# A two-block transformer kernel on one core: attention mask by short products, recurrent splits and mixes moved, first unit of three feed-forward stages reordered

## The reference

```python
for layer in range(2):
    if layer == 1:
        k_shared, v_shared = shared_kv(x, ...)
    x = x + 0.5 * swiglu(rmsnorm(x, ffn1_norm[layer]), w_gate, w_up, w_down)    # 1024 -> 2816 -> 1024
    h = rmsnorm(x, mix_norm[layer])
    if layer == 0:
        x = x + recurrent_block(h, ...)
    else:
        x = x + diff_attention(h, k_shared, v_shared, ...)
    x = x + 0.5 * swiglu(rmsnorm(x, ffn2_norm[layer]), w_gate, w_up, w_down)

def recurrent_block(h, ...):
    gate, rec = split(h @ w_in)
    rec = rg_lru(causal_depthwise_conv(rec))      # h_t = a_t h_{t-1} + bx_t
    return (gelu(gate) * rec) @ w_out

def diff_attention(...):                          # 8 heads, each with two score maps
    scores = q @ k.T                              # blocks of 128 queries
    mask = key // 64 <= query // 64
    p = softmax(where(mask, scores, -inf))
    attn = p[:, 0] - lam * p[:, 1]
    return rmsnorm(attn @ v) @ w_o
```

## Time and profile before

| | us |
|---|---|
| median of 3 executions (3706.11 to 3715.54) | 3709.11 |
| the profiled execution, whole | 3714.02 |
| its span, first to last instruction | 3712.7 |
| PE busy in the span | 3600.5 |
| DVE busy | 2471.0 |
| ACT busy | 1601.6 |
| POOL busy | 288.2 |
| mean granted clock of PE | 0.977 of full speed |

### The profile page before, as it was taken

How to read it: one execution, slowest core, us unless ns; L and a number is a source line. 1 busy time by engine, 2 the same in 40 slices (tenths; PEclk the granted TensorE clock), 3 DMA queues, 4 the chain that set the end, 5 groups by cost and what they waited for, 6 DMA issues and landing times.

```text
span 3712.7 us, 53317 instructions
## 1 busy us (share of the span) xinstructions
PE 3600.5 (97%) x21504; PEld 3067.0 (83%) x21504; DVE 2471.0 (67%) x3699; ACT 1601.6 (43%) x2579; POOL 288.2 (8%) x245
## 2 busy tenths in 40 slices
PE   8999999999999998999999999999999999979999
PEld 5866788888888866888899986899978999659998
DVE  6455767755547265544688877888756887478886
ACT  3246733323135234422454446544444444475443
POOL 0001005820000011000000011000020000110000
PEclk8999999999999899999999999999999999999999
DMA  6200032333322101222333322233323334203332
GB/s 227 96 23 1 2 103 88 128 126 125 125 78 75 57 29 57 91 97 97 97 96 104 109 91 78 87 105 103 105 87 126 108 103 148 64 18 103 104 105 89
DMA packets 276455, 338.96 MB, mean 91 GB/s; under 512 B 15601, under 2 KB 197489, under 8 KB 275569
## 3 DMA queue, kind: packets, MB, share of 16 engines
q1 hardware_dynamic: 272752, 320.40, 27.5%
q10 hardware_dynamic: 3456, 15.14, 1.1%
HBM read 329.19 MB, written 6.29 MB: 90 GB/s over the span
## 4 chain that ended last, share of the span: by engine, by line
PE 82%; DVE 7%; ACT 2%; issue 2%; DMA 0%; POOL 0%; SPq 0%; ACTq 0%; DVEq 0%
PE ps L862 15%; PE ps L864 15%; PE ps L863 15%; PE ps L1788 7%; PE ps L1790 7%; PE ps L1789 7%; PE ps L2274 1%; PE ps L2248 1%; PE ps L2133 1%; PE ps L2134 1%; PE ps L2135 1%; DVE t L443 1%; PE ps L2238 1%; PE ps L877 1%; PE ps L879 1%
## 5 line engine op out<-in xcount | busy, mean ns | idle before, releaser
L862 PE MATMUL ps<-t 128*128 128x512 f32 (+1 forms) x2188 | 789.9, 361 | 4.0 <-DVE t L3840 2.7
L863 PE MATMUL ps<-t 128*128 128x512 f32 (+1 forms) x2188 | 785.6, 359 | 0.0
L864 PE MATMUL ps<-t 128*128 128x512 f32 (+1 forms) x2188 | 784.5, 359 | 0.0
L430 ACT ACTIVATE t<-t 128x1024 fp32r<-128x1024 f32 (+2 forms) x438 | 437.1, 999 | 566.6 <-PE ps L864 331.1
L443 DVE TENSOR_TENSOR t<-t 128x1024 fp32r<-128x1024 f32 (+2 forms) x438 | 505.8, 1156 | 244.3 <-ACT t L430 241.7
L1788 PE MATMUL ps<-blocks_hi,t 128*128 128x256 f32 x1888 | 533.0, 282 | 15.0 <-ACT t L1817 11.7
L1790 PE MATMUL ps<-blocks_hi,t 128*128 128x256 f32 x1888 | 528.6, 280 | 0.0
L1789 PE MATMUL ps<-blocks_lo,t 128*128 128x256 f32 x1888 | 528.6, 280 | 0.0
L862 PEld LDWEIGHTS ps<-t 128*128 128x128 f32 x2188 | 418.7, 191 | 67.3 <-issue 4.0
L863 PEld LDWEIGHTS ps<-t 128*128 128x128 f32 x2188 | 418.8, 191 | 60.2 <-issue 1.0
L864 PEld LDWEIGHTS ps<-t 128*128 128x128 f32 x2188 | 418.2, 191 | 60.7
(11 more groups left out here) (514 smaller groups left out, 6326.0 us busy)
## 6 DMA issues: line engine op xcount, KB each, us to landing
t<-w_s_up SPq DMA_DIRECT2D x184, 256.0 KB, 3.6
t<-w_up SPq DMA_DIRECT2D x88, 512.0 KB, 3.6
raw_more<-w_s_up SPq DMA_DIRECT2D x168, 256.0 KB, 3.4
t<-w_ada SPq DMA_DIRECT2D x160, 256.0 KB, 3.1
raw_more<-w_s_down SPq DMA_DIRECT2D x72, 256.0 KB, 2.7
t<-w_down SPq DMA_DIRECT2D x32, 512.0 KB, 3.6
t<-w_s_down SPq DMA_DIRECT2D x56, 256.0 KB, 2.7
t<-w_ada SPq DMA_DIRECT2D x16, 512.0 KB, 11.0
```

Source lines behind the costliest of these rows:

```text
L430: k.A.activation(self.pair(n)[0], self.slot(self.raw_at[n])[:, 0:self.size(n)], ACT.Copy)\
L862: k.T.matmul(out, wh, hh, start=(i == 0), stop=False)
L863: k.T.matmul(out, wh, hl, start=False, stop=False)
L864: ins = k.T.matmul(out, wl, hh, start=False, stop=(i == len(kts) - 1))
```

## The change

1. Attention: the memset and its semaphore go. After the two score products PE adds two short products into the corner of each map: 64 rows by 64 columns, a constant 0/1 matrix cut from the constants (`early_rows`) times a column of -2^94 read 64 times, which adds -2^100 for queries 0 to 63. The ratio is a `scalar_tensor_tensor` in place of a `tensor_scalar` with two scalars from memory.
2. Recurrent stage, i from 9: `dve_scans` gives a new order, in which the splits of chunks 13 to 17 and the last norms come between single scans; the split of chunk 13 on ACT lies between the two square roots; all mixes but the first move behind the last projection, each ahead of one low part, and the last two `dve_normed` (14 and 15) go there too. `rec_out` takes the paired form.
3. Blocks of the first unit in s_up10, s_up20 and s_up21 (s_up11 is not `summed` and keeps its order). DVE at tile 6: sum S2 comes right behind t1, the residual of tile 7 ahead of `dve_add(5)`; at tile 7 the differences first, then S2's low part, spans 2 and 1, `dve_add(6)`; in the stage itself A12's low part ahead of `dve_add(7)`. ACT: S2's high part right behind tile 6's square; `act_keep(0, 0)` ahead of span 1's high part; then A12's, the square of tile 7 and a small Sqrt activation that loads the table ahead of the root.

```diff
@@ -1269,8 +1270,6 @@
         k, (p, odd) = self.k, divmod(m, 2)
         for t in free:
             k.act.wait_ge(t)
-        if m == 6 and self.summed:
-            k.stream.split_hi(self.first)
         k.act.wait_ge(self.finished(m, 0))
         k.act.wait_ge(self.at("beside", 4 * p))
         k.act.wait_ge(self.low(p - 1, 1 if odd else 0))
@@ -1280,17 +1279,18 @@
             self.act_hi(p, 1)
         elif odd:
             self.act_hi(p, 2)
-            if self.summed:
-                k.stream.split_hi(self.first + 2)
-            self.act_hi(p, 1)
         else:
             if p:
                 self.act_hi(p - 1, 2)
             self.act_hi(p, 0)
             if m == 6 and self.summed:
                 k.stream.split_hi(self.first + 1)
-        if self.summed:
+        if self.summed and m < 7:
             self.act_square(m)
+        if m == 6 and self.summed:
+            k.stream.split_hi(self.first + 2)
+        if m == 7 and not self.summed:
+            self.act_hi(p, 1)
...
-    def dve(self, m, free=()):
+    def dve(self, m, free=(), last=None):
         k, st, (p, odd) = self.k, self.k.stream, divmod(m, 2)
         for t in free:
             k.dve.wait_ge(t)
         if not self.summed:
             self.dve_blocks(m)
+            if last:
+                last()
         elif m == 7:
+            self.dve_t234(p)
+            st.split_lo(self.first + 2)
+            self.dve_lo(p, 2)
+            self.dve_lo(p, 1)
             self.dve_add(6)
-            self.dve_t234(p)
-            st.sum(self.up, 0, "S2")
-            self.dve_lo(p, 2)
-            st.split_lo(self.first + 2)
-            self.dve_lo(p, 1)
         elif odd:
             self.dve_add(m - 1)
             self.dve_t234(p)
             self.dve_lo(p, 1)
-        else:
-            if m == 6:
-                st.sum(self.up, 0, "S1")
-            elif m:
+        elif m < 6:
+            if m:
                 self.dve_add(m - 1)
             self.dve_t1(p)
-            if m == 6:
-                st.split_lo(self.first)
             self.dve_lo(p, 0)
-            if m == 6:
-                st.split_lo(self.first + 1)
             if p:
                 self.dve_lo(p - 1, 2)
-            if m == 6:
-                self.dve_add(m - 1)
+        else:
+            st.sum(self.up, 0, "S1")
+            self.dve_t1(p)
+            st.sum(self.up, 0, "S2")
+            self.dve_lo(p, 0)
+            self.dve_lo(p - 1, 2)
+            st.split_lo(self.first + 1)
+            last()
+            self.dve_add(5)
...
+                if isinstance(feed, BlockFeed) and g == 2 and j == 7:
+                    feed.dve(6, [vd.at(ns * FT)], lambda: dve_residual(g, j))
+                    continue
...
                             act_silu(j, 0)
                         if j == 0 and q == 3 and source.summed:
                             source.act_root()
+                        if j == 0 and q == 0 and source.summed:
+                            act_keep(0, 0)
+                            source.act_hi(3, 1)
                         st.split_hi(st.look(c + q))
+                        if j == 0 and q == 0 and source.summed:
+                            source.act_square(7)
+                            k.A.activation(k.SM[:, 103:104], k.eps(EPS), ACT.Sqrt)
                         if j == 0 and q == 4 and source.summed:
                             source.act_rstd()
-                        if q < 3:
+                        if q < 3 and not (j == 0 and q == 0 and source.summed):
                             act_keep(j, q)
                         if q == 0 and left is not None:
...
                         if q > 3:
                             dve_even(j, q)
                         if j == 0 and q == 0 and source.summed:
+                            st.split_lo(c + 3)
                             source.dve_add(7)
                         if q == 0:
                             st.split_lo(c + 1)
...
+            if isinstance(self.feed, BlockFeed) and m == 7:
+                self.feed.dve(6, (), lambda: self.dve_residual(7))
+                continue
...
                     k.act.wait_ge(m2.at(4 * half + 4))
                     k.A.activation(v, v, ACT.Sqrt).then_inc(mu.sem, 1)
+                    if half == 0:
+                        st.split_hi(c0 + 13)
...
                     m = i % 8
-                    st.split_hi(c0 + i + 2)
+                    if i < 9:
+                        st.split_hi(c0 + i + 2)
...
-                    if 8 <= i < 15:
+                    if 8 <= i < 14:
                         act_gelu(m)
+                        st.split_hi(c0 + min(i + 5, 17))
...
+            def dve_normed(i):
+                k.dve.wait_ge(md.at(i + 1))
+                k.dve.wait_ge(ri.at(i - 1) if i < 10 else gl.at(i - 9))
+                k.V.tensor_tensor(normed(i), bank[i], RS, ALU.mult).then_inc(sc.sem, 1)
+
+            def dve_scans():
+
+                for i, scans, split in ((9, (0,), 13), (None, (1,), None), (10, (2,), 14), (11, (3, 4), 15), (12, (5,), 16),
+                                        (13, (6,), 17), (None, (7,), None)):
+                    if i:
+                        dve_normed(i)
+                    for m in scans:
+                        dve_scan(m)
+                    if split:
+                        st.split_lo(c0 + split)
+                    if i == 13:
+                        dve_mix(0)
...
-                    for m in {9: (0, 1, 2), 10: (3,), 11: (4,), 12: (5,), 13: (6,), 14: (7,)}.get(i, ()):
-                        dve_scan(m)
-                    for m in {10: (0,), 11: (1,), 12: (2,), 13: (3,), 14: (4,), 15: (5, 6)}.get(i, ()):
-                        dve_mix(m)
+                dve_scans()
...
-        out = ProjectOut(k, "rec_out", [MX], lambda si, kt: hl.at(kt + 1), lambda m, si: 1.0, None, following)
+        out = ProjectOut(k, "rec_out", [MX], lambda si, kt: hl.at(kt + 1), lambda m, si: 1.0, None, following, True)
...
             for m in range(8):
                 if m == 2:
+                    act_gelu(6)
                     act_gelu(7)
...
             k.dve.wait_ge(h_free)
             for m in range(8):
-                if m == 2:
-                    dve_mix(7)
+                if m < 7:
+                    dve_mix(m + 1)
+                if m in (1, 2):
+                    dve_normed(13 + m)
...
         for c in range(2):
             r = slice(64 * c, 64 * c + 64)
-            ins = k.T.matmul(k.ps[:, 2 * (i % 2) + c, 0:self.nk(i)], self.Q[r, h, q * 128:(q + 1) * 128],
-                             self.KS[r, h, 0:self.nk(i)], start=True, stop=True)
+            k.T.matmul(k.ps[:, 2 * (i % 2) + c, 0:self.nk(i)], self.Q[r, h, q * 128:(q + 1) * 128],
+                       self.KS[r, h, 0:self.nk(i)], start=True, stop=False, skip_group_check=True)
+        for c in range(2):
+            ins = k.T.matmul(k.ps[:, 2 * (i % 2) + c, self.nk(i) - 64:self.nk(i)], k.early_rows[c],
+                             k.SM[64 * c:64 * c + 64, 3:4].broadcast_to([64, 64]), start=False, stop=True, skip_group_check=True)
         ins.then_inc(self.sc.sem, 1)
 
...
         k, nk, m, (h, q), s = self.k, self.nk(i), self.small(i), self.pairs[i], 2 * (i % 2)
         k.dve.wait_ge(self.factor_ready(h))
         k.dve.wait_ge(self.sc.at(i + 1))
-        k.V.memset(k.ps[0:64, s:s + 2, nk - 64:nk], -1e30).then_inc(self.hid.sem, 1)
-        k.dve.wait_ge(self.hid.at(i + 1))
         k.V.tensor_reduce(m[:, 0:2], k.ps[:, s:s + 2, 0:nk], AX.X, ALU.max).then_inc(self.mx.sem, 1)
         k.dve.wait_ge(self.mx.at(i + 1))
...
-        k.V.tensor_scalar(m[:, 0:1], m[:, 7:8], self.neg_lam, m[:, 4:5], ALU.mult, ALU.mult).then_inc(self.ratio.sem, 1)
+        k.V.scalar_tensor_tensor(out=m[:, 0:1], in0=m[:, 7:8], scalar=self.neg_lam, in1=m[:, 4:5], op0=ALU.mult, op1=ALU.mult)\
+            .then_inc(self.ratio.sem, 1)
```

55 lines of the change are left out of this document (30 added, 25 removed).

## The result

The changed kernel took 3682.3 us (median of four runs, 3679.0 to 3687.1) beside 3707.6 for the kernel before: ratio 0.9929, 95% interval 0.9917 to 0.9942, that is 21.5 to 30.8 us less. The forecast was 3689.3, 19.8 us less, a ratio of 0.9947: the direction was right and the gain too small. The two profiled executions have spans of 3712.7 and 3685.7 us.

The account below looks back on a forecast made before the run. PE, busy 97% of the span, was taken as the bound, with DVE setting the end of first-unit stretches and bounding attention; 9.9 + 5.9 + 4.0 = 19.8 us off 3709.1 gave 3689.3 us, range 3682 to 3702.

Parts of the forecast that it names:

- First units, 9.9: s_up10, s_up20 and s_up21: the new order removes DVE's waits and gains 4.0, 2.7 and 3.2 us, 9.9 in all.
- Recurrent stage, 5.9: Recurrent stage: removing PE's wait before i = 13 gains 6.7 us, less 0.8 for the clock, so 5.9; bounds 4 and 7.
- The two waits inside the pair: Paired start of `rec_out`: PE waits 0.4 us at kt = 1 and 1.65 at kt = 2.
- Attention, 4.0: Attention: a head becomes 9.72 us for 10.26, so eight heads gain about 4.0 us after the first masks; bounds 0.5 and 6.
- the memset is 0.165 and its semaphore 0.035: Attention: the removed memset costs DVE 0.165 us and its semaphore 0.035, four times per head; two memsets return 0.40.
- 2.66 plus 0.21 is as long as the old chain and memset: Attention, q = 3: PE's chain with the mask takes 2.87 us, the old chain and memset 2.86, so this step gains nothing.
- The ratio's 0.22: Attention: the ratio's new form takes 0.22 us on DVE in place of 0.273; three ratios return 0.15 per head.
- the mask's 0.21: Attention: the mask's four short passes cost PE 0.21 us, between 0.1 and 0.58.
- (a): Rival: new waits take over in first units and the pair, and the clock falls after each; gain 9.5, 3699.6 us; chance 15%.
- (b): Rival: DVE isn't the bound behind L1873 and PE's time comes through too; gain 26 us, 3683; chance 10%.
- (c): Rival: attention's short products cost a fixed price, 0.32 us a pass to undo the other gains; slower than before; chance 4%.
- (d): Rival: the order fails, for example a high part behind a load stops DVE in all three first units; 3699 us; chance 6%.

Follow-up runs that it names:

- e9: The kernel before with only the new order of the first unit in the three seven-product stages (and the blocks feeding it): ratio 0.9974 to the kernel before.
- e11: The changed kernel with ACT issuing the root ahead of S4's high part and storing the norm earlier: first-unit stretches 30.80, 28.18 and 28.18 us for 31.76, 29.13 and 29.12.
- e1: The kernel before with only the attention change: ratio 0.9970 to the kernel before, a steady head 9.38 us for 10.26.
- e5: The changed kernel with the old PSUM memset put back ahead of the reduction, beside the mask products: a head at full clock took 10.26 us.
- e4: The changed kernel with each pair of mask products in attention issued twice: a head took 9.61 us for 9.39.

## Why the prediction was right in places, and where it was wrong

The forecast's 19.8 us lies below the measured interval of 21.5 to 30.8. The step that failed is the price of the mask in attention: what the memset costs DVE, and what the short products add to PE's chain.

- **First units, 9.9.** Measured 10.2, alone (e9) as in the whole. The way to it held too: in s_up10 PE's product 3 began 7.29 us behind product 1 (7.2 forecast), its next waits are 0.63 and 1.28 for 0.6 and 1.6, and DVE's waits of 0.19, 0.84 and 0.78 stand where 0.2, 1.0 and 0.65 were put. DVE was the bound by 0.41 us, where 1.1 was said, and e11 showed that it is.
- **Recurrent stage, 5.9.** Measured 5.8, and 6.2 alone, both against a profile in which the clock was low for 13.7 us; against the three with 10.2 it is 4.6 and 4.9, and 5.0 by the means. So 5.9 is rather too much, and that it met 5.8 is in part luck. No wait before i = 13, 4.88 before `rec_out` for 5.1. The two waits inside the pair, 0.4 and 1.65, didn't come as waits: PE worked through them at its lower clock.
- **Attention, 4.0.** Measured 6.1 in e1, 7.2 in the whole (both profiles of the changed kernel), 7.0 by the means. The mechanism was right: DVE bounds three steps of four, PE's chain the fourth. Two terms were mis-sized. The step "the memset is 0.165 and its semaphore 0.035" left out the overlap of 0.10 that the next operation regains: a memset between two DVE operations costs 0.30, as e5 shows (the reduction starts 0.56 behind the result for 0.26). Rows like those above could have been read in the trace of before. That is 0.20 a head. And the step "2.66 plus 0.21 is as long as the old chain and memset" counted the start of the memset behind PE's last pass as if a reduction needed it too, and the mask at its full length where it overlaps the last score pass: 0.10 a head. With these the head is 0.54 + 0.20 + 0.10 = 0.84 shorter; 0.88 was measured. The ratio's 0.22 (0.225 measured, mean of 32) and the mask's 0.21 (0.22 in e4) were right. The Trainium skill, VectorE: DVE Perf Modes, section on the TRN2 errata, has a formula for a tensor_tensor, by which one column would take an estimated 158 ns. The trace's tensor_tensor of two columns, 165 ns, is near it; the scalar_tensor_tensor of one column took 225, so the formula doesn't carry over to this form.
- **What is left.** The touched stages give 4.1 + 5.8 + 2.7 + 3.3 + 6.1 = 22.0 us, and 4.0 + 5.0 + 3.0 + 3.2 + 7.0 = 22.2 by the means; the timed ratio says 21.5 to 30.8. Forecast plus the 2.1 missing in attention would be within that interval at its lower end. That the middle lies 4 us higher isn't shown to belong to the change: the code ahead of s_up10, untouched, took 1836.4 (e9) to 1847.9 us (before) in the profiles of this study, and the kernel before happened to be the longest. It stays open.
- **Rivals.** (a) didn't come: s_up10 has the three new waits in a row, s_up20 and s_up21 only one of 1.1 for the spread, and the clock stayed full in all three. (b) fell with e11. (c) fell with e4: 0.055 us a pass, not 0.32. (d): no split in the new order waited for a load.

## What to carry to other kernels

Price an operation that goes not by its busy time but by the distance between the starts of its neighbours with and without it; the trace of before shows both, wherever the same neighbour once stands behind another kind of operation. A wait that becomes shorter matters only up to the next engine that is late, so lay the new order on measured durations, engine by engine, and look for the engine that is last at the end of the stretch. When one step of a loop is fed by a chain, look first for work in that chain which its end doesn't need: moving the scores ahead of the values brought as much per head, 0.86 us, as the whole change of attention.

## What the hardware showed that had not been expected

- A memset on DVE doesn't overlap the end of the operation ahead of it as others do. Behind the result of attention, into PSUM it starts 0.00 to 0.02 us behind that end, into SBUF 0.03 to 0.05 ahead of it, a copy or a reduction 0.08 to 0.09 ahead. Behind a PE pass a memset into PSUM started 0.10 us after it, a reduction 0.05.
- Waits of 0.6 to 1.3 us within 10 us of PE's work (s_up10 above) left the granted clock at full, and it was full there in all 13 profiles with the new order of the unit; in the five with the old order, each with one wait of 5.4, it was low for 6.8 us.
- The clock was also low for 3.41 us where PE has no wait (2774.74, the third window above). What PE did before it fell is six passes on 16 rows:

```profile
2770.84 2.84 PE L4025 MATMUL ps<-t 16*128 16x512 f32 x6
```

They end at 2773.68, 1.06 us ahead of the fall. 8 of this study's 18 profiles have such a low stretch, each beginning between 0.4 us ahead of the end of such a group and 1.1 behind it; the other 10 ran the same passes and have none. So the same work is followed by either level, and two executions of one kernel differ by it: the changed kernel's first profile has a low stretch in s_up11 too and takes 31.09 us there, its second has none and takes 30.75.
